# Token tiles of 640 columns in place of 644: a DiT layer with attention and RWKV-7 on one core

## The reference

```python
h = modulate(rmsnorm(x, norm1_g), shift1, scale1)
q, k, v, u, ga, gr = split(h @ w_in)
q, k = rmsnorm(q, q_norm_g), rmsnorm(k, k_norm_g)      # per head of 64
# latent: rotary on q and k; keys and values are the latent ones and 256 cached ones
attn = softmax(q @ k.T / 8) @ v                        # 8 heads, 2 key heads
u = dwconv3(u, rwkv_conv)                              # width 3, zeros beyond both ends
r, k, v, wd, ad, gd = split(u)
kk = k * k_k; kk = kk * rsqrt(sum(kk * kk) + 1e-12)    # per head: the "key norm"
y = wkv7_scan(forward) + wkv7_scan(backward)           # data-dependent decay, 64 x 64 state
merged = sigmoid(ga) * (attn @ w_attn_br) + sigmoid(gr) * (rwkv(y) @ w_rwkv_br)
x = x + gate1 * (merged @ w_out)
up_u, up_g = split(dwconv3(modulate(rmsnorm(x, norm2_g), shift2, scale2) @ ffn_up, ffn_conv))
x = x + gate2 * ((silu(up_g) * up_u) @ ffn_down)
return rmsnorm(x, final_norm_g), new keys, new values, final states
```

## Time and profile before

| | us |
|---|---|
| median of 3 runs | 1372.39 |
| lowest, highest | 1363.66, 1373.96 |
| the profiled execution, its own time | 1366.4 |
| its span from first to last instruction | 1364.6 |
| PE busy in the span | 1286.1 |
| DVE, ACT, POOL busy | 688.9, 549.9, 42.1 |

### The profile page before, as it was taken

One profiled execution on the slowest core, in us unless ns is written; L12 is line 12 of the kernel. 1 busy time (PEld: TensorE's weight loads), 2 busy tenths in 40 slices (PEclk: granted clock), 3 DMA queues, 4 the chain that ended last, 5 costly groups with the idle time before them and its releaser, 6 DMA issues.

```text
span 1364.6 us, 31724 instructions
## 1 busy us (share of the span) xinstructions
PE 1286.1 (94%) x13903; PEld 1190.8 (87%) x13903; DVE 688.9 (50%) x1036; ACT 549.9 (40%) x864; POOL 42.1 (3%) x103
## 2 busy tenths in 40 slices
PE   4899999999999868999999999899999999999995
PEld 1899999998999554489989878799999999999995
DVE  3427652752544676565556412554554545533544
ACT  3635534432223577633342221733433334333433
POOL 0100011000010000000000000000000000000000
PEclk9899999999999989999999999899999999999998
DMA  9422265315000200010017484022121221022222
GB/s 391 147 72 100 101 250 183 137 40 212 17 5 4 93 1 1 0 54 11 32 42 256 178 359 173 32 77 77 61 92 61 66 88 38 24 77 73 69 74 93
DMA packets 24027, 131.70 MB, mean 97 GB/s; under 512 B 2896, under 2 KB 3664, under 8 KB 15344
## 3 DMA queue, kind: packets, MB, share of 16 engines
q1 hardware_dynamic: 19104, 103.98, 21.7%
q0 software_dynamic: 4816, 26.11, 5.1%
HBM read 111.74 MB, written 18.34 MB: 95 GB/s over the span
## 4 chain that ended last, share of the span: by engine, by line
PE 86%; DVE 4%; ACT 3%; DMA 3%; issue 1%; PEld 1%; SPq 0%; PEldq 0%; DVEq 0%; ACTq 0%
PE ps L714 47%; PE ps L1229 11%; PE ps L884 4%; PE ps L872 4%; PE ps L852 2%; DMA adaw<-in_wada 2%; PE ps L1095 1%; PE ps L864 1%; PE ps L739 1%; PE ps L998 1%; PEld ps L739 1%; PE ps L758 1%; PE ps L749 1%; DMA adl<-in_wada 1%; DVE nmax L1995 1%
## 5 line engine op out<-in xcount | busy, mean ns | idle before, releaser
L714 PE MATMUL ps<-h2lo,whi 128*128 128x322 f32 x672 | 154.5, 311 | 0.7 <-ACT facc L1331 0.7
L714 PE MATMUL ps<-h2hi,wlo 128*128 128x322 f32 x672 | 155.0, 312 | 0.0
L714 PE MATMUL ps<-h2hi,whi 128*128 128x322 f32 x672 | 154.0, 310 | 0.0
L1683 DVE TENSOR_TENSOR wlo<-raw,whi 128x2048 fp32r<-128x2048 f32 x47 | 107.5, 2287 | 75.4 <-ACT whi L1292 75.4
L714 PE MATMUL ps<-hlo,whi 128*128 128x322 f32 x544 | 127.9, 316 | 1.0 <-ACT qkv L1357 1.0
L714 PE MATMUL ps<-hhi,wlo 128*128 128x322 f32 x544 | 125.4, 312 | 0.0
L714 PE MATMUL ps<-hhi,whi 128*128 128x322 f32 x544 | 124.7, 310 | 0.0
L714 PEld LDWEIGHTS ps<-h2hi,whi 128*128 128x128 f32 x672 | 114.1, 190 | 0.0
L714 PEld LDWEIGHTS ps<-h2lo,whi 128*128 128x128 f32 x672 | 113.0, 189 | 0.9 <-issue 0.9
L714 PEld LDWEIGHTS ps<-h2hi,wlo 128*128 128x128 f32 x672 | 113.6, 189 | 0.0
L1730 DVE SCALAR_TENSOR_TENSOR facc<-fraw,par,facc 128x642 f32<-128x642 f32 x44 | 39.0, 887 | 138.5 <-ACT facc L1331 138.5
(11 more groups left out here) (353 smaller groups left out, 2584.3 us busy)
## 6 DMA issues: line engine op xcount, KB each, us to landing
raw<-in_wblk SPq DMA_DIRECT2D x48, 1024.0 KB, 4.9
adl<-in_wada SPq DMA_DIRECT2D x8, 2048.0 KB, 8.1
raw<-in_wdn SPq DMA_DIRECT2D x44, 256.0 KB, 2.6
adaw<-in_wada SPq DMA_DIRECT2D x4, 2048.0 KB, 20.7
gate_scratch<-gout POOLq DMA_DIRECT2D x16, 322.0 KB, 2.6
gld<-gate_scratch POOLq DMA_DIRECT2D x8, 644.0 KB, 5.0
attention_inputs_used<-attention_scratch SPq DMA_DIRECT2D x1, 5056.0 KB, 15.4
u_scratch<-uout POOLq DMA_DIRECT2D x12, 320.0 KB, 2.4
```

The costliest lines, as they stand in the source:

```text
L714: mm = pe.matmul(o, w, v, start=first, stop=last and w is hi and x is xh[n])
L1683: TT(wlo[s][:, :], raw[s][:, :], whi[s][:, :].bitcast(F32), ALU.subtract).then_inc(lo_done, 1)
```

## The change

Tiles lose their zero columns: `TP` becomes 640, `L0` 0 and `C0` 512, so that each product of 322 columns has 320, and `FLAT` becomes 192. The zeros stay in the buffers that the convolutions read (`craw`, `fraw`, `CW` = 643 columns, borders written once each by `borders`); `conv_evac` copies latent and context part in two instructions, `convolve` issues two instructions for either outer tap. The zeroing of `hf`, `rwo` and of the branch tiles (24 memsets of GpSimd, and TensorE's wait for them) goes, and `rwo` is written in one instruction. Inputs and outputs in DRAM have 640 columns too.

In the attention: the first key sum's product is issued after step 16 and not 17, VectorE copies both sums (steps 17 and 21) and not only the first, ScalarE makes the first norm in step 20, with the logarithms of half of the denominators, and the second norm in the first step of the key scores. VectorE writes two of the first four rows of denominators in steps 27 and 29 and the others after step 31, in place of four in steps 27 to 30.

```diff
@@ -33,8 +33,10 @@
-TP = 644
-L0, C0 = 1, 514
+TP = T
+L0, C0 = 0, 512
+CONV = ((0, 512, 0), (512, 128, 513))
+CW = T + 3
@@ -236,10 +239,11 @@
     spot[0] = h_end
-    craw = [sb(f"craw{s}", [P, TP]) for s in range(2)]
+    craw = [sb(f"craw{s}", [P, CW]) for s in range(2)]
     cacc = [sb(f"cacc{s}", [P, TP]) for s in range(2)]
...
     gout = [sb(f"gout{s}", [P, TP]) for s in range(2)]
+    spot[0] += 64
     def attention_inputs(at, name):
@@ -683,11 +687,6 @@
             gp.dma_start(staged[s], br_s[s]).then_inc(b_ld[s], 16)
-        for x in (bhi, blo):
-            for k in range(4):
-                for a, n in ((0, 1), (L0 + LAT, 1), (C0 + CTX, 2)):
-                    gp.memset(x[k][:, a:a + n].bitcast(F32), 0.0).then_inc(pads_set, 1)
-        gp.wait_ge(pads_set, 24)
         presets(1)
@@ -1116,7 +1115,7 @@
                 context_values()
-            if n == 17:
+            if n == 16:
                 pe.wait_ge(o_copied, 1)
@@ -1146,7 +1145,6 @@
         pe.wait_ge(b_lo, 4)
-        pe.wait_ge(pads_set, 24)
         pe.wait_ge(lo_done, BLK_BR + 1)
@@ -1219,13 +1217,13 @@
                 hi, lo = (w[0 if second else s][:, at:at + P] for w in (whi, wlo))
-                outs = out_halves(2 * f, TP - 2)
+                outs = out_halves(2 * f)
                 if again:
...
                 for q, (w, x) in enumerate(((hi, xl), (lo, xh), (hi, xh))):
-                    for o, v in zip(outs, halves(x, TP - 2)):
+                    for o, v in zip(outs, halves(x)):
                         mm = pe.matmul(o, w, v, start=(k == 0 and q == 0), stop=(k == FF - 1 and q == 2))
@@ -1327,7 +1325,8 @@
                 ac.wait_ge(conv_done, conv_k)
-            ac.activation(fr[j][:, :], tile(2 * j), ACT.Copy)
+            for a, w, at in CONV:
+                ac.activation(fr[j][:, at + 1:at + 1 + w], tile(2 * j)[:, a:a + w], ACT.Copy)
             ac.activation(fa[j][:, :], tile(2 * j), ACT.Identity, scale=wcol).then_inc(tile_evac, 1)
@@ -1519,11 +1518,6 @@
                 key_squares(1)
-            elif 2 <= i < 4:
-                key_norm_log(1, i - 2)
-            elif i == 4:
-                for s in range(2):
-                    key_norm(1, s)
             elif i >= 5:
@@ -1543,6 +1537,16 @@
 
+        def second_key_log(s):
+            rn = (tbs[1][1], tbs[1][8])[s][:, :]
+            ac.wait_ge(prep_read, 13 + s)
+            ac.activation(rn, rn, ACT.Ln, bias=1e-12).then_inc(key_logs, 1)
+
+        def second_key_norm(s):
+            rn = (tbs[1][1], tbs[1][8])[s][:, :]
+            ac.wait_ge(key_logs, s + 1)
+            ac.activation(rn, rn, ACT.Exp, scale=-0.5).then_inc(ac_prep, 1)
+
         for n in range(32):
@@ -1551,14 +1555,10 @@
                 between_heads(1)
-            if n == 21:
-                ac.wait_ge(prep_read, 13)
-                ac.activation(tbs[1][1][:, :], tbs[1][1][:, :], ACT.Ln, bias=1e-12)
-                key_norm_log(1, 1)
+            if n == 20:
+                second_key_log(0)
                 denominator_logs(0)
-                ac.wait_ge(prep_read, 14)
-                for s in range(2):
-                    key_norm(1, s)
+                second_key_norm(0)
         for s in range(2):
@@ -1572,6 +1572,8 @@
                 denominator_logs(1)
+                second_key_log(1)
+                second_key_norm(1)
             for i in head_ticks(z):
@@ -1682,10 +1684,12 @@
 
-        def borders(t):
-
-            for a, n in ((0, 1), (L0 + LAT, 1), (C0 + CTX, 2)):
-                dv.memset(t[:, a:a + n], 0.0)
+        def borders(ts):
+
+            for t in ts:
+                for a in (0, LAT + 1, CW - 1):
+                    ins = dv.memset(t[:, a:a + 1], 0.0)
+            st.last(ins)
 
@@ -1722,22 +1724,24 @@
         phase_over(dv, 1)
-
-
-        def convolve(n, j, taps, fr, fa, outs):
+        borders(craw)
+
+
+        def convolve(n, j, taps, fr, fa, dst):
 
             dv.wait_ge(tile_evac, n + 3)
-            st.last(STT(fa[j][:, 1:TP - 1], fr[j][:, 0:TP - 2], taps(0), fa[j][:, 1:TP - 1], ALU.mult, ALU.add))
-            for a, w, o in outs:
-                ins = STT(o, fr[j][:, a + 1:a + 1 + w], taps(2), fa[j][:, a:a + w], ALU.mult, ALU.add)
+            for a, w, at in CONV:
+                ins = STT(fa[j][:, a:a + w], fr[j][:, at:at + w], taps(0), fa[j][:, a:a + w], ALU.mult, ALU.add)
+            st.last(ins)
+            for a, w, at in CONV:
+                ins = STT(dst[:, a:a + w], fr[j][:, at + 2:at + 2 + w], taps(2), fa[j][:, a:a + w], ALU.mult, ALU.add)
             ins.then_inc(conv_done, 1)
...
                 dv.wait_ge(u_st[j], wait_stored)
-            convolve(n, j, lambda q: pc("rconv", 3 * t + q), craw, cacc,
-                     ((L0, LAT, dst[:, 0:LAT]), (C0, CTX, dst[:, LAT:T])))
+            convolve(n, j, lambda q: pc("rconv", 3 * t + q), craw, cacc, dst)
 
@@ -1956,9 +1959,7 @@
                 dv.wait_ge(pe_e[s], 4 * it + 4)
-                for a, w, c in ((0, LAT, L0), (LAT, CTX, C0)):
-                    ins = TT(rwo[s][:, c:c + w], psf[:, at + 1024 + a:at + 1024 + a + w], y[:, a:a + w], ALU.mult)
-                ins.then_inc(rwo_done, 1)
+                TT(rwo[s][:, :], psf[:, at + 1024:at + 1024 + T], y, ALU.mult).then_inc(rwo_done, 1)
 
@@ -2055,13 +2056,16 @@
                 context_out()
-            if n == 18:
-                dv.wait_ge(pe_prep, 11)
-                dv.tensor_copy(tbs[1][1][:, :], psf[:, 3072:3072 + T]).then_inc(prep_read, 1)
+            if n in (17, 21):
+                s = (n - 17) // 4
+                dv.wait_ge(pe_prep, 11 + s)
+                dv.tensor_copy((tbs[1][1], tbs[1][8])[s][:, :], psf[:, 3072:3072 + T]).then_inc(prep_read, 1)
             if n == 23:
                 lse_columns(0)
-            if 27 <= n < 31:
-                lse_row(n - 27)
+            if n in (27, 29):
+                lse_row((n - 27) // 2)
+        for h in (2, 3):
+            lse_row(h)
         for z in range(12):
@@ -2109,9 +2113,6 @@
                 next_lo(BLK_OUT + 2 + o // 2, (o // 2) % 2)
-            if o == 5:
-                for s in range(2):
-                    dv.memset(hf[s][:, :], 0.0)
             if o == 6:
@@ -2120,6 +2121,7 @@
         modulate(1, x1, h2hi, h2lo, 0)
+        borders(fraw)
         dv.wait_ge(modt_done, 11)
@@ -2127,7 +2129,7 @@
             for j, dst in ((0, fcu), (1, fcg)):
-                convolve(2 * b + j, j, lambda q, j=j: pc("fconv", 6 * j0 + 3 * j + q), fraw, facc, ((1, TP - 2, dst[:, :]),))
+                convolve(2 * b + j, j, lambda q, j=j: pc("fconv", 6 * j0 + 3 * j + q), fraw, facc, dst)
             if split:
@@ -2168,7 +2170,7 @@
                 for c, (a, w) in enumerate(((L0, LAT), (C0, CTX))):
-                    ins = STT(x1[:, o, a:a + w], tile(2 * f)[:, a - 1:a - 1 + w], g2h[:, o, c:c + 1], x1[:, o, a:a + w],
+                    ins = STT(x1[:, o, a:a + w], tile(2 * f)[:, a:a + w], g2h[:, o, c:c + 1], x1[:, o, a:a + w],
                               ALU.mult, ALU.add)
...
```

More of the change, by code:

```diff
@@ L216, in build @@
     rs = sb("rs", [P, TP])
+    spot[0] += 256
     xr = [sqf + xr4, sqf]
@@ L286, in build @@
     late_tb = spot[0]
-    assert late_tb <= qa_at
+    assert late_tb + 2 * 32 * ((4 * NC * (CH + 1) + 31) // 32) <= qa_at
     spot[0] = qa_at
@@ L369, in build @@
     af_at = spot[0]
-    af = sb("af", [P, FF, TP - 2])
+    af = sb("af", [P, FF, TP])
     spot[0] = after_ring
-    fraw = [sb(f"fraw{s}", [P, TP]) for s in range(2)]
+    fraw = [sb(f"fraw{s}", [P, CW]) for s in range(2)]
     facc = [sb(f"facc{s}", [P, TP]) for s in range(2)]
[L374 to L377, removed]
+    fcu = sb("fcu", [P, TP])
+    fcg = sb("fcg", [P, TP])
+    ftg = sb("ftg", [P, TP])
+    dhi, dlo = [sb("dhi0", [P, TP], F32R)], [sb("dlo0", [P, TP], F32R)]
     assert spot[0] <= norm_end
     spot[0] = x1_end
-    dhi.append(sb("dhi1", [P, TP - 2], F32R))
-    dlo.append(sb("dlo1", [P, TP - 2], F32R))
+    dhi.append(sb("dhi1", [P, TP], F32R))
+    dlo.append(sb("dlo1", [P, TP], F32R))
     ysq = [sb(f"ysq{k}", [P, TP]) for k in range(KD)]
@@ L384, in build @@
     spot[0] = raw_at + 4 * 512
-    dhi_second, dlo_second = (sb(name, [P, TP - 2], F32R) for name in ("dhi_second", "dlo_second"))
+    dhi_second, dlo_second = (sb(name, [P, TP], F32R) for name in ("dhi_second", "dlo_second"))
     assert spot[0] <= raw_at + 4 * WEL
@@ L453, in build @@
     low_done = sem("decay_gate_inputs")
-    prep_read = sem("prep_products_read")
+    prep_read, key_logs = sem("prep_products_read"), sem("key_sums_logs")
     pe_prep, ac_prep, dv_prep = sem("prep_products"), sem("prep_scalar"), sem("prep_vector")
@@ L469, in build @@
     b_ld = [sem(f"rwkv_again_loaded{s}") for s in range(2)]
-    pads_set, half_hi = sem("branch_pads_zero"), sem("half_of_branch_weights_hi")
+    half_hi = sem("half_of_branch_weights_hi")
     gl_ld = [sem(f"gates_loaded{s}") for s in range(2)]
@@ L1945, in epilogue @@
                 at = 4 * s * 512
-                borders(rwo[s])
```

## The result

The changed kernel takes 1356.06 us (median of 4 runs, 1348.64 to 1359.45) against 1369.5 us before (4 runs, 1363.66 to 1373.96): a ratio of 0.9892, 95% interval 0.9855 to 0.9928. That is 13 to 15 us less, where the sum of the prediction had 5.9. The two traces must therefore be read by stage, and not by their ends. Where a price is given for the first or the second half of a tile, it is the mean time from the start of one product to the start of the next, over the single products of the trace without the few that wait.

A forecast was written before the change was run, and what follows sets the result against it. TensorE's dense products in the projections were taken as the bound. Terms -4.5 (columns), -1.6 (attention), +0.55 (copies, convolutions) and -0.3 (RWKV output) sum to -5.9 us; between 1360.5 and 1366.5, 1363.5 was taken, range 1351 to 1372.

The forecast's parts named there:

- starts matter: Rival in the projections: where second halves start in their tile sets the excess step; time near 1354 us, chance 0.10.
- the columns' term: Up- and down-projection: 5136 products get 320 columns in place of 322, 0.88 ns less each, -4.5 us.
- Weights set the step: Rival in the projections: weight loads, not columns, set 0.149 us a product; 4.5 us stay out, 1368 us, chance 0.08.
- The attention's term: Five edits of the attention's order together: -1.6 us, with ends at +3 and -4.9.
- (b): Row scores: the first norm's product moves ahead one row and waits for the context's output, +0.7 us.
- (a): ScalarE's block in the row scores: one logarithm and one of two exponentials leave it, -1.3 us.
- (d): End of the row scores: two of four rows of denominators go behind the last maximum, -1.6 us.
- (e): First keys: the second norm's logarithm and exponential now stand between ScalarE's two table loads, +1.4 us.
- (c): Behind ScalarE's block in the row scores: the half-clock stretch begins later or ends earlier, -0.8 us.
- Copies and convolutions: More instructions per evacuation and convolution: +0.15 us at the first block after the norm, +0.4 at the down-projection's turn, sum +0.55.
- The clock rival: A longer pause before the key scores brings further half-clock stretches, 1.7 us each; with five 1372 us, chance 0.05.
- half clock in the key scores beyond one stretch: Sign in the attention's key scores: if the clock is at half there beyond one stretch, the forecast is wrong.

The follow-up runs named there:

- before336: The kernel before with its tile of 644 columns cut at 336 and 308 in place of 322 and 322; ratio 0.9965.
- oldatt: The changed kernel with all five attention edits undone; 1355.83 us, ratio 0.9906.
- newatt: The kernel before with the five attention edits alone; 1366.08 us, ratio 0.9991.
- rows4: The changed kernel with four rows of denominators in steps 27 to 30 again; 1352.03 us, ratio 0.9885.
- prod17: The changed kernel with only the first key sum's product put back behind step 17; 1352.5 us, ratio 0.9876.
- half322: The changed kernel with its 640 columns cut at 322 and 318, so the second half starts 1288 bytes in; 1362.87 us, ratio 0.9975.
- base8: The changed kernel with the up-projection's input tiles placed 8 bytes off in memory; 3.6 us more in the piece of 2016 products.
- base16: The changed kernel with the up-projection's input tiles placed 16 bytes off in memory; 295.68 us for the 2016 products.
- space: The changed kernel with larger up-projection input tiles, 2592 bytes apart, used from their first byte; 295.67 us for the 2016 products.

## Why the prediction was right and where it was wrong

**The range and the direction** held: 1356 lies between 1351 and 1372, and the kernel is faster. The likeliest value, 1363.5, was too high, the change being 13 to 15 us and not 5.9. The forecast's own range, 1356 to 1369, holds the result only at its edge; what came is the case of the rival "starts matter", which had 1354 and a chance of 0.10. That the range held is owed to that rival and not to the sum.

**The step that failed is the columns' term: it put the start of the operand at nothing.** Its slope was nearly right. It gave 0.88 ns for two columns, and before336 shows 0.9. But 149.0 ns was taken as the time of 322 columns, and half of those products had a start 1288 bytes into their tile, which makes their step 150.0 and not 147.8. The working had seen that 322 lies above the other sizes and gave this to the rival. By halves the sum comes out: 5136 products x 0.92 ns = 4.7 us for the columns, about the 4.5 of the working, and 2832 second halves (those of the 5136, and the 528 of the down-projection that kept 320 columns) x 2.3 ns = 6.5 us for the start, which the sum had as 0. Together 11.2; by the step of all 5664, at 2.2 ns, it is 12.5. oldatt, which has these terms with the copies and nothing else, measures 12.9 (9 to 16). The trace of before could have told, as its own single starts show first and second halves of 322 columns 2.2 ns apart.

**"Weights set the step"** is out: the step fell with the loads unchanged, and the halves of 308 columns in before336, each with its own load, have a step of 141.4 ns.

**The attention's term**, -1.6 us, is -1.8 by the pieces of newatt and before, and the time, -1.2 us (with 3.7 less to 1.1 more), agrees. Its parts hold as well. (b) was +0.7 and is +0.9. (a) with the pause, 4.12 in place of 5.32 us in all kernels with the new order, was -1.3 and is most of -1.6. (d) was -1.6 and is -1.8 by rows4. (e) was +1.4 and is +1.3 on ScalarE. TensorE's pause in the first keys was to grow from 2.85 to 4.2 and is 3.0 where the clock is at full ahead of it (newatt, prod17), 2.63 in the changed kernel: behind the late rows TensorE arrives there 1.1 us later after the first key exponentials than before (newatt), so that the pause doesn't show the cost. (c), -0.8 for the clock behind the block, is seen where the stretch at half lasts 3.4 and not 6.8 us: 8.1 us to the first keys in newatt, 9.0 in prod17 and half322. What (c) missed is that the clock falls at other places of the attention, and for other lengths, from trace to trace of nearly the same instructions.

**Copies and convolutions**: +0.4 at the turn to the down-projection. The pause grew by 2.5 - 2.1 = 0.4, the chain that ends it by 0.3: the convolutions are 0.26 as forecast, the copies 0.06 and not 0.15. At the first block after the norm two copies take 0.77 where the earlier trace rows had 0.71 for one, and the path from there to the next product is 1.59 us in place of 1.54 (883.65 - 882.11 in the earlier trace rows): 0.05, not 0.15.

**The clock rival** came in part. One of the prediction's own signs of being wrong, half clock in the key scores beyond one stretch, did show (517.9 to 524.6 and 565.6 to 569.0 us of the changed kernel), and so the stretch that was to be 1 to 3 us shorter is 4.4 longer in that trace. It was wrong in its reach: stretches at half also came in the row scores, ahead of both pauses, and no experiment's median is above before. Its price, 1.7 us for a stretch of 3.4, is about what the down-projection shows, 72.13 - 70.60 = 1.5 us. The clock is also part of why runs of one kernel lie 10 us apart: in the four runs of the changed kernel, 1348.64, 1354.64, 1357.48 and 1359.45 us go with mean clocks of 0.985, 0.982, 0.981 and 0.98. But 0.005 of the mean is some 14 us more at half, which costs 7 at most, and the ends lie 10.8 apart; the rest is open.

## What to carry to other kernels

When a product is made narrower, look at where its operand starts as well as at how many columns it has: here a moving fp32r operand 8 bytes past a multiple of 16 cost more, and one 16 bytes past a multiple of 32 didn't, so cut tiles at a multiple of 16 bytes. Before taking a slope from products of several sizes, check that they are alike in all else, and compare products of one size with each other: if they differ, something other than the size has a price. Where the granted clock moves a stage by several microseconds, an edit of one microsecond is read piece by piece, between marks at which both traces do the same. Added work in a pause of TensorE must end before the pause does; then the pieces behind it get shorter, by about 1 us each here.

## What the runs showed of the hardware

A moving fp32r operand of 320 columns that starts 8 bytes past a multiple of 16 costs 1.8 ns more, 148.6 in place of 146.8 ns (base8); 16 bytes past a multiple of 32 costs nothing (base16, 295.68 us for 2016 products against 295.67 in space). Among well-placed products a column costs 0.46 ns (before336, 154.2 ns for 336 and 141.4 for 308). An fp32 product of 512 columns is issued as two, 0.43 us from start to start at full clock (eight in 3.70 us, to the modelled end of the last). With added products in a pause the granted clock was at full behind it, in all three traces that have them. The clock fell to half at 1186.8 us in the changed kernel, after a pause of 2.18 us in work that is dense on either side; after the same pause in base8 it stayed at full.
